# Row-tiled scatter and four-slot weight DMAs in the expert loop of a hybrid encoder layer with MoE

## Chip, cores and metric

One core of one Trainium2 chip. The metric is the device time of one launch in microseconds (us); lower is better. The kernel before has a median of 1183.3 us over 3 runs (1180.84 to 1186.23).

## What is computed

One layer on 256 tokens of width 1024, all in float32: RMSNorm, a mixer (projection, causal convolution, a complex linear recurrence, gates, output projection), then a top-4-of-32 mixture of experts, then a final RMSNorm. The change lies in the mixture of experts, which the reference gives per expert as:

```
gu = xb @ w_gate_up[e] + b_gate_up[e]            # (rows, 1024) @ (1024, 2048)
g, lin = gu[:, :1024], gu[:, 1024:]
g = jnp.minimum(g, 7.0); lin = jnp.clip(lin, -7.0, 7.0)
act = g * jax.nn.sigmoid(1.702 * g) * (lin + 1.0)
y = act @ w_down[e] + b_down[e]                  # (rows, 1024) @ (1024, 1024)
out[token] += gate[token, e] * y[row of token]
```

The weights of one expert are 8 MiB (w_gate_up) and 4 MiB (w_down); 32 experts make 384 MiB.

## The kernel before

Everything before the experts (mixer, router) takes about the first 270 us. After that comes a loop of 16 iterations with two experts each (`half` is 0 or 1), written out by hand in one order per engine; semaphores join the engines.

**The ring.** All weights pass through `ring`, 24 slots of 1 MiB (8 KiB in each of 128 partitions), 12 slots (`PER`) for each half. Slots 0 to 7 of a half hold one contraction block k of w_gate_up each, slots 8 to 11 hold two k of w_down each. The first two experts are loaded slot by slot ahead of the loop (`load`). Inside it SyncE (SP) waits for each two slots until the matmuls that read them have counted `chunk_used` up, and issues one DMA of 2 MiB for the expert two further on (`load_pair`, L355 to L361, called at L414 to L416); each pair of slots has a semaphore `pair_in`.

**TensorE (PE) for expert e** (L1316 to L1333): bias matmuls (L1272), `gate_up` for k = 0 to 3 (L1280), `gather` for the next expert (L1253, picks its tokens by a one-hot product), `gate_up` for k = 4 to 7, then `scatter` (L1298 to L1301), which adds the result of the expert before, `yrow`, to the output in PSUM banks 0 to 3, then `transposes` (L1259) of the activated rows `gc` and of the gathered rows, `spread_transposes` (L1264), and `down` (L1292). An expert has 64 rows. So that they use all 128 partitions of the outputs, gate_up, gather and down are column tiled: two matmuls with 64 columns each, `h` = 0 and 1, write partitions 0 to 63 and 64 to 127 of one bank, and the two run side by side. `yrow` therefore holds output columns 0 to 511 of the 64 rows in partitions 0 to 63 and columns 512 to 1023 in partitions 64 to 127. The scatter multiplies it with `spT`, the transposed matrix of gates. `spT` has a plane for each half of the columns, with zeros in the 64 partitions that belong to the other half, so each of the four matmuls (bank n: tokens n // 2, columns n % 2) runs over all 128 partitions.

**VectorE (DVE)** waits at L998 until gate_up is finished, clips the two halves (L969, L972), writes `spread` (L964), and makes the product (L975, L978). With L978 it releases PE's wait for `act_ready` at L1326. **ScalarE (ACT)** does the sigmoid (L658), copies PSUM to SBUF (L646, L649, L652, L655) and copies `spT` in two instructions (L662, L663), one for each 64 partitions.

After the loop PE scatters the last expert (L1366 to L1369), and ACT, DVE and SP make the final norm and store the output. A branch for experts with more than 64 rows (L1334 to L1363) is never entered with these inputs.

Of the kernel before, what the change touches and what calls it, by code (L numbers as in the profile page):

```python
# [26 lines left out]
D = 1024  # L27
T = 256
# [34 lines left out]
def build(nc, x, norm_mix_g, w_in, conv_w, conv_b, conv_ln_g, conv_ln_b, w_conv_out,  # L63
# [3 lines left out]
    with ExitStack() as ctx:  # L67
# [80 lines left out]
        gate = sb("gate", [128, TT, E + 1])  # L148
        pick = sb("pick", [128, TT, CAP])
        spread = sb("spread", [128, TT, 2, CAP])  # L150
        spT = sb("spT", [128, 2, TT, 128])
        biasb = sb("biasb", [96, 4 * 512], BF16)
        esel = sb("esel", [96, E + 1], BF16)
        onehot = sb("onehot", [96, 2, CAP], BF16)
# [43 lines left out]
        ffn_in = sem("ffn_in")  # L198
        down_in = sem("down_in")
        fin_in = sem("fin_in")  # L200
        pair_in = [sem(f"pair_in{i}") for i in range(SLOTS // 2)]
        stored = sem("stored")
        dve_own = sem("dve_own")
        pool_own = sem("pool_own")
# [102 lines left out]
        def _(sp):  # L307
# [38 lines left out]
            def load(e, j, half):  # L346

                if j < KD:
                    src, dst = gu_v[e, :, j, :], at(half * PER + j, CH)
                else:  # L350
                    c = j - KD
                    src, dst = dn_v[e, c // 2, :, c % 2 * 2:c % 2 * 2 + 2, :], grid(at(half * PER + j, CH), 2, D)
                sp.dma_start(dst, src).then_inc(pair_in[(half * PER + j) // 2], 16)

            def load_pair(e, j, half):  # L355

                if j < KD:
                    src, dst = gu_v[e, :, j:j + 2, :], grid(at(half * PER + j, 2 * CH), 2, CH)
                else:
                    src, dst = dn_v[e, (j - KD) // 2], grid(at(half * PER + j, 2 * CH), 4, D)  # L360
                sp.dma_start(dst, src).then_inc(pair_in[(half * PER + j) // 2], 16)  # L361

            sp.wait_ge(y_pe, ST)
            sp.dma_start(gffn, norm_ffn_g.to_broadcast([128, D])).then_inc(ffn_in, 16)
# [40 lines left out]
            with sp.Fori(0, E // 2 - 1) as i:  # L405
                for half in range(2):
                    e = i * 2 + half
                    with sp.If(any_more > 0):
                        over = sp.value_load(nums[0:1, bass.ds(e, 1)], min_val=0, max_val=1)
                        with sp.If(over > 0):  # L410
                            before = sp.value_load(nums[0:1, bass.ds(e + E, 1)], min_val=0, max_val=E)
                            sp.wait_ge(step, before * MORE_STEPS + MORE_STEPS + 1)
                            sp.sem_inc(passed, 1)
                    for j in range(0, PER, 2):  # L414
                        sp.wait_ge(chunk_used, e * PER + j + 2)
                        load_pair(e + 2, j, half)  # L416
            sp.wait_ge(chunk_used, E * PER - PER)
            sp.dma_start(at(0, D), norm_final_g.unsqueeze(0).to_broadcast([128, D])).then_inc(fin_in, 16)
            for t in range(TT):
# [7 lines left out]
        def _(pool):  # L427
# [99 lines left out]

            g.memset(rank[:, :, E:E + 1], -1.0).then_inc(consts, 1)
            g.memset(gate[:, :, E:E + 1], 0.0).then_inc(consts, 1)
            g.memset(spT[:, :, :, :], 0.0).then_inc(spT_sb, 1)  # L530
            pool.wait_ge(y_pe, ST)
            g.memset(ones, 1.0).then_inc(consts, 1)
            link(g.memset(tri, 1.0))
# [6 lines left out]
        def _(act):  # L540
# [118 lines left out]

            def spread_copy():  # L660

                s.activation(spT[0:64, 0, :, :], grid(bank[5][0:64, 0:T], 2, 128), ACT.Copy)  # L662
                return s.activation(spT[64:128, 1, :, :], grid(bank[5][64:128, 0:T], 2, 128), ACT.Copy)  # L663

            act.wait_ge(h_pe, 1)
            h_row_copy().then_inc(h_row, 1)
# [373 lines left out]
        def _(pe):  # L1040
# [226 lines left out]
            def gate_up(half, buf, part=None, uses=None):  # L1267

                ks = range(KD) if part is None else range(4 * part, 4 * part + 4)
                for b in range(2 if 0 in ks else 0):  # L1270
                    for h in range(2):
                        mm(bank[4 + b][64 * h:64 * h + 64, :], onehot[:, buf, :], biasb[:, (2 * b + h) * 512:(2 * b + h + 1) * 512],  # L1272
                           start=True, stop=False)
                for k in ks:
                    if uses is not None and k % 2 == 0:
                        pe.wait_ge(pair_in[(half * PER + k) // 2], uses)
                    w = at(half * PER + k, CH)
                    for b in range(2):
                        for h in range(2):
                            last = mm(bank[4 + b][64 * h:64 * h + 64, :], heT[:, k % 4, k // 4 * 64:k // 4 * 64 + 64],  # L1280
                                      w[:, b * FF + h * 512:b * FF + h * 512 + 512], start=False, stop=(k == KD - 1))
                    if uses is not None:
                        last.then_inc(chunk_used, 1)
                return last

            def down(half, uses=None):
                for k in range(KD):
                    if uses is not None and k % 4 == 0:
                        pe.wait_ge(pair_in[(half * PER + KD + k // 2) // 2], uses)
                    w = grid(at(half * PER + KD + k // 2, CH), 2, D)  # L1290
                    for h in range(2):
                        last = mm(bank[6][64 * h:64 * h + 64, :], actT[:, k % 4, k // 4 * 64:k // 4 * 64 + 64],  # L1292
                                  w[:, k % 2, h * 512:h * 512 + 512], start=(k == 0), stop=(k == KD - 1))
                    if uses is not None and k % 2:
                        last.then_inc(chunk_used, 1)
                return last

            def scatter():  # L1298
                for n in range(4):
                    last = mm(bank[n][:, :], spT[:, n % 2, n // 2, :], yrow, start=False, stop=False, skip_group_check=True)  # L1300
                return last  # L1301

            pe.wait_ge(gmT_sb, 1)
# [11 lines left out]
            with pe.Fori(0, E // 2) as i:  # L1315
                for half in range(2):  # L1316
                    e = i * 2 + half
                    pe.wait_ge(h_T, e + 1)
                    pe.wait_ge(spT_sb, e + 1)
                    gate_up(half, half, 0, i * 16 + 32)  # L1320
                    pe.wait_ge(pick_ready, e + 2)
                    pe.wait_ge(y_row, e + 1)
                    gather().then_inc(h_pe, 1)
                    gate_up(half, half, 1, i * 16 + 32)
                    scatter()
                    pe.wait_ge(act_ready, e + 1)  # L1326
                    transposes(gc, 4).then_inc(aT_pe, 1)
                    pe.wait_ge(h_row, e + 2)
                    transposes(hrow, 7).then_inc(hT_pe, 1)
                    pe.wait_ge(spread_ready, e + 1)  # L1330
                    spread_transposes().then_inc(spT_pe, 1)
                    pe.wait_ge(a_T, e + 1)
                    down(half, i * 16 + 32)  # L1333
                    with pe.If(any_more > 0):  # L1334
                        over = pe.value_load(nums[0:1, bass.ds(e, 1)], min_val=0, max_val=1)
                        with pe.If(over > 0):
                            before = pe.value_load(nums[0:1, bass.ds(e + E, 1)], min_val=0, max_val=E)
                            pe.wait_ge(y_row, e + 2)
                            pe.sem_inc(passed, 1)
                            with pe.Fori(0, MORE) as b:  # L1340
                                o = before * MORE_STEPS + b * BLOCK_STEPS + 1
                                pe.wait_ge(step, o)
                                scatter().then_inc(step, 1)
                                pe.wait_ge(step, o + 2)
                                gather().then_inc(step, 1)
                                pe.wait_ge(step, o + 4)
                                transposes(hrow, 7)
                                spread_transposes().then_inc(step, 1)
                                pe.wait_ge(step, o + 6)
                                gate_up(half, half).then_inc(step, 1)  # L1350
                                pe.wait_ge(step, o + 11)
                                transposes(gc, 4).then_inc(step, 1)
                                pe.wait_ge(step, o + 13)
                                down(half).then_inc(step, 1)
                            a = before * MORE_STEPS + MORE * BLOCK_STEPS + 1
                            pe.wait_ge(step, a)
                            scatter().then_inc(step, 1)
                            pe.wait_ge(step, a + 2)
                            gather().then_inc(step, 1)
                            pe.wait_ge(step, a + 4)  # L1360
                            transposes(hrow, 7).then_inc(step, 1)
                            pe.wait_ge(step, a + 6)
                            pe.sem_inc(passed, 1)  # L1363
            pe.wait_ge(y_row, E + 1)
            pe.wait_ge(spT_sb, E + 1)
            for t in range(TT):  # L1366
                for h in range(2):
                    last = mm(bank[2 * t + h][:, :], spT[:, h, t, :], yrow, start=False, stop=True, skip_group_check=True)
                last.then_inc(x2_pe, 1)  # L1369


# [18 lines left out]
```

## Time and profile before

| | |
|---|---|
| median of 3 runs | 1183.3 us (1180.84 to 1186.23) |
| the profiled execution, its own time | 1182.04 us |
| its span, first to last instruction | 1180.2 us |
| PE busy | 1126.3 us, 95% |
| DVE, ACT, POOL busy | 316.7, 179.1, 95.8 us |
| moved by DMA | 431.89 MB, mean 366 GB/s |
| mean granted TensorE clock | 0.972 of 2.4 GHz |

The profile is of one execution, and all times in it count from the first instruction. Its own time is 1.8 us above its span. Matmul records have modelled ends and overlap each other; starts are what to compare. A busy engine is not by itself the bound: what counts is which wait ends last in the stretch in question. "Granted clock" is 1.00 for 2.4 GHz and 0.50 for 1.2 GHz.

### The profile page before, as it was taken

The numbers are of one execution on the slowest core, as the hardware profiler recorded it, in microseconds if no ns is written. First come the engines' busy times: TensorE is split into PE (matmuls) and PEld (weight loads), VectorE is DVE, ScalarE is ACT, GpSimd is POOL, SyncE is SP. The second block draws the span as 40 slices with busy tenths as digits, with TensorE's granted clock in tenths as the row PEclk, the third lists the DMA queues.
The fourth block names the chain that finished last, engine by engine and source line by source line (L and its number), as shares of the span: only waits on it lengthen the run. The fifth ranks groups of instructions, "written<-read, shape, count | busy, mean of one in ns | idle before, by whom it ended". The sixth has DMA issues, their size and how long they took to land.

```text
span 1180.2 us, 12748 instructions
## 1 busy us (share of the span) xinstructions
PE 1126.3 (95%) x4959; PEld 497.7 (42%) x4960; DVE 316.7 (27%) x661; ACT 179.1 (15%) x333; POOL 95.8 (8%) x155
## 2 busy tenths in 40 slices
PE   7977769989999999999999999999999999999997
PEld 6855658553333333333333333333333333333332
DVE  3999996131111111111111111111111111111112
ACT  3100113111111111111111111111211111111112
POOL 2992520000000000000000000000000000000000
PEclk9987889979999999999999999999999999999999
DMA  8834018957999999999999999999999999999994
GB/s 230 255 98 179 1 38 350 386 214 294 411 416 419 428 429 428 429 429 428 428 429 429 428 429 428 429 428 428 428 429 429 428 429 429 429 428 428 428 429 206
DMA packets 51619, 431.89 MB, mean 366 GB/s; under 512 B 6466, under 2 KB 22256, under 8 KB 25391
## 3 DMA queue, kind: packets, MB, share of 16 engines
q1 hardware_dynamic: 51598, 431.62, 88.2%
q8 instruction: 12, 0.20, 0.1%
q14 instruction: 9, 0.07, 0.0%
HBM read 430.56 MB, written 1.05 MB: 366 GB/s over the span
## 4 chain that ended last, share of the span: by engine, by line
PE 81%; DVE 11%; DMA 5%; SPq 2%; issue 1%; ACT 1%; DVEq 0%; POOL 0%
PE bank L1280 34%; PE bank L1292 18%; PE bank L1300 9%; DVE ring L812 7%; PE bank L1253 4%; DMA ring<-w_gate_up 4%; PE bank L1259 3%; PE bank L1078 3%; PE bank L1215 2%; PE bank L1180 2%; SPq L361 1%; PE bank L1272 1%; DVE ring L844 1%; DVE ring L845 1%; DVE ring L835 1%
## 5 line engine op out<-in xcount | busy, mean ns | idle before, releaser
L1280 PE MATMUL bank<-ring,area 128*64 128x512 f32 x2048 | 451.7, 593 | 0.3 <-DMA ring<-w_gate_up 0.3
L1280 PEld LDWEIGHTS bank<-ring,area 128*64 128x64 f32 x2048 | 147.3, 137 | 281.5 <-issue 274.8
L969 DVE TENSOR_SCALAR area<-bank 128x512 f32<-128x512 f32 x32 | 22.1, 692 | 769.4 <-PE bank L1280 769.4
L1292 PE MATMUL bank<-ring,area 128*64 128x512 f32 x1024 | 226.8, 595 | 1.0
L1292 PEld LDWEIGHTS bank<-ring,area 128*64 128x64 f32 x1024 | 70.6, 137 | 136.6 <-issue 128.0
L1300 PE MATMUL bank<-area,spT 128*128 128x512 f32 x256 | 118.4, 605 | 0.0
L1078 PE MATMUL bank<-area,ring 128*128 128x256 f32 x480 | 116.8, 406 | 1.2 <-DVE area L749 1.2
L1078 PEld LDWEIGHTS bank<-area,ring 128*128 128x128 f32 x480 | 97.7, 206 | 20.4 <-issue 3.6
L812 DVE SCALAR_TENSOR_TENSOR ring<-ring,spread 128x256 f32<-128x256 f32 x180 | 98.3, 620 | 0.0
L658 ACT ACTIVATE area<-area 128x512 f32<-128x512 f32 x32 | 20.1, 630 | 497.3 <-DVE area L969 497.3
L1300 PEld LDWEIGHTS bank<-area,spT 128*128 128x128 f32 x256 | 46.0, 189 | 71.9 <-issue 71.9
L1253 PE MATMUL bank<-rows,pick 128*64 128x512 f32 x264 | 63.6, 604 | 0.0
L655 ACT ACTIVATE area<-bank 128x512 f32<-128x512 f32 x32 | 19.1, 597 | 193.7 <-PE bank L1292 193.7
L1259 PEld LDWEIGHTS bank<-ident,area 128*128 128x128 f32 x260 | 27.8, 141 | 26.0 <-DVE area L978 25.2
L1253 PEld LDWEIGHTS bank<-rows,pick 128*64 128x64 f32 x264 | 19.2, 139 | 39.3 <-issue 39.3
L1259 PE MATMUL bank<-ident,area 128*128 128x128 f32 x260 | 35.6, 280 | 0.0
L978 DVE TENSOR_TENSOR area<-area 128x512 f32<-128x512 f32 x32 | 33.7, 1053 | 1.1
L652 ACT ACTIVATE area<-bank 128x512 f32<-128x512 f32 x32 | 19.1, 597 | 76.7 <-PE bank L1259 76.7
L1215 PE MATMUL bank<-ring 128*128 128x512 f32 x64 | 28.1, 594 | 0.0
L1095 PE MATMUL bank<-area,ring 32*128 32x256 f32 x32 | 9.5, 480 | 17.0 <-ACT ring L584 17.0
L1272 PE MATMUL bank<-biasb,onehot 96*64 96x512 bf16 x128 | 19.8, 387 | 2.6 <-issue 2.6
L975 DVE SCALAR_TENSOR_TENSOR area<-area 128x512 f32<-128x512 f32 x32 | 21.9, 684 | 0.0
(240 smaller groups left out, 575.0 us busy)
## 6 DMA issues: line engine op xcount, KB each, us to landing
ring<-w_gate_up SPq DMA_DIRECT2D x120, 2048.0 KB, 29.9
ring<-w_down SPq DMA_DIRECT2D x60, 2048.0 KB, 28.3
ring<-w_gate_up SPq DMA_DIRECT2D x16, 1024.0 KB, 12.0
ring<-w_in SPq DMA_DIRECT2D x15, 1024.0 KB, 9.6
ring<-w_down SPq DMA_DIRECT2D x8, 1024.0 KB, 13.1
ring<-w_out SPq DMA_DIRECT2D x1, 4096.0 KB, 14.0
ring<-w_conv_out SPq DMA_DIRECT2D x1, 3072.0 KB, 13.3
rows<-x SPq DMA_DIRECT2D x2, 512.0 KB, 3.7
```

What stands on the lines that cost most here:

```text
L812: ins = v.scalar_tensor_tensor(conv[:, k, :], src, taps[:, k, w:w + 1], conv[:, k, :], ALU.mult, ALU.add)
L969: return v.tensor_scalar(gc, bank[4][:, :], 7.0, None, ALU.min)
L978: return v.tensor_tensor(gc.rearrange("a (m p) -> a p m", p=128), grid(lc, 128, 4), grid(sg, 128, 4), ALU.mult)
L1078: last = mm(bank[4 + n % 4][:, m * T:m * T + T], w[:, k, m * 128:m * 128 + 128], hT[:, k, :], start=(k == 0), stop=(k == KD - 1))
L1180: last = mm(bank[4 + j][:, m * T:m * T + T], wconv[:, k, c:c + 128], silu[:, k, :], start=(k == 0), stop=(k == KC - 1))
L1215: last = mm(bank[2 * t + h][:, :], gateC[:, k, t * 128:t * 128 + 128], wout[:, k, h * 512:h * 512 + 512], start=False, stop=(k == KD - 1))
L1253: last = mm(bank[6][64 * h:64 * h + 64, :], pick[:, t, :], rows[:, t, h * 512:h * 512 + 512], start=(t == 0), stop=(t == TT - 1))
L1259: last = tr(bank[b][:, m * 128:m * 128 + 128], src[:, m * 128:m * 128 + 128], ident[:, :])
L1272: mm(bank[4 + b][64 * h:64 * h + 64, :], onehot[:, buf, :], biasb[:, (2 * b + h) * 512:(2 * b + h + 1) * 512], start=True, stop=False)
L1280: last = mm(bank[4 + b][64 * h:64 * h + 64, :], heT[:, k % 4, k // 4 * 64:k // 4 * 64 + 64], w[:, b * FF + h * 512:b * FF + h * 512 + 512] ...
L1292: last = mm(bank[6][64 * h:64 * h + 64, :], actT[:, k % 4, k // 4 * 64:k // 4 * 64 + 64], w[:, k % 2, h * 512:h * 512 + 512], start=(k == ...
L1300: last = mm(bank[n][:, :], spT[:, n % 2, n // 2, :], yrow, start=False, stop=False, skip_group_check=True)
```

## The change

1. In the loop SP waits for four slots and issues one DMA of 4 MiB: k = 0 to 3, then k = 4 to 7 of w_gate_up (32 KiB in one run for each partition, 16 KiB before), then the whole w_down of the expert (two runs of 16 KiB for each partition). PE waits for four slots at a time, on `quad_in`.
2. `spT` has one plane of 128 partitions without zeros; ACT copies it with one instruction.
3. The scatter is row tiled: bank n uses only the 64 partitions of `spT` and `yrow` that hold its columns, 0 to 63 for even n and 64 to 127 for odd n. The final scatter does the same.

```diff
-        spT = sb("spT", [128, 2, TT, 128])
+        spT = sb("spT", [128, TT, 128])
...
-            def load_pair(e, j, half):
+            def load_quad(e, j, half):
 
                 if j < KD:
-                    src, dst = gu_v[e, :, j:j + 2, :], grid(at(half * PER + j, 2 * CH), 2, CH)
+                    src, dst = gu_v[e, :, j:j + 4, :], grid(at(half * PER + j, 4 * CH), 4, CH)
                 else:
-                    src, dst = dn_v[e, (j - KD) // 2], grid(at(half * PER + j, 2 * CH), 4, D)
-                sp.dma_start(dst, src).then_inc(pair_in[(half * PER + j) // 2], 16)
+                    src, dst = dn_v[e].rearrange("h p m n -> p h m n"), grid(at(half * PER + j, 4 * CH), 2, 4, D)
+                sp.dma_start(dst, src).then_inc(quad_in[(half * PER + j) // 4], 16)
...
-                    for j in range(0, PER, 2):
-                        sp.wait_ge(chunk_used, e * PER + j + 2)
-                        load_pair(e + 2, j, half)
+                    for j in range(0, PER, 4):
+                        sp.wait_ge(chunk_used, e * PER + j + 4)
+                        load_quad(e + 2, j, half)
...
-                s.activation(spT[0:64, 0, :, :], grid(bank[5][0:64, 0:T], 2, 128), ACT.Copy)
-                return s.activation(spT[64:128, 1, :, :], grid(bank[5][64:128, 0:T], 2, 128), ACT.Copy)
+                return s.activation(spT[:, :, :], grid(bank[5][:, 0:T], 2, 128), ACT.Copy)
...
-                    if uses is not None and k % 2 == 0:
-                        pe.wait_ge(pair_in[(half * PER + k) // 2], uses)
+                    if uses is not None and k % 4 == 0:
+                        pe.wait_ge(quad_in[(half * PER + k) // 4], uses)
...
-                    if uses is not None and k % 4 == 0:
-                        pe.wait_ge(pair_in[(half * PER + KD + k // 2) // 2], uses)
+                    if uses is not None and k == 0:
+                        pe.wait_ge(quad_in[half * 3 + 2], uses)
...
+            def scatter_half(n, stop=False):
+
+                r = slice(n % 2 * 64, n % 2 * 64 + 64)
+                return mm(bank[n][:, :], spT[r, n // 2, :], yrow[r, :], start=False, stop=stop, skip_group_check=True)
+
             def scatter():
                 for n in range(4):
-                    last = mm(bank[n][:, :], spT[:, n % 2, n // 2, :], yrow, start=False, stop=False, skip_group_check=True)
+                    last = scatter_half(n)
...
-                    last = mm(bank[2 * t + h][:, :], spT[:, h, t, :], yrow, start=False, stop=True, skip_group_check=True)
+                    last = scatter_half(2 * t + h, stop=True)
```

On SP, the six DMAs of an expert in the loop become three. Before:

```order
L361 ISA
L361 DMA ring<-w_gate_up 128x4096
L415 REGISTER_ALU
L361 ISA
L361 DMA ring<-w_gate_up 128x4096
...
L361 ISA
L361 DMA ring<-w_down 128x4096
L415 REGISTER_ALU
L361 ISA
L361 DMA ring<-w_down 128x4096
```

and now (each "ISA" row here is the wait for `chunk_used`):

```order
L361 ISA
L361 DMA ring<-w_gate_up 128x8192
L415 REGISTER_ALU
L361 ISA
L361 DMA ring<-w_gate_up 128x8192
L415 REGISTER_ALU
L361 ISA
L361 DMA ring<-w_down 128x2x4096
```

The order of the rows is the same; each DMA has moved behind the wait for two more slots.

## Rows read from the trace of the kernel before

**Rows 1.** The page: busy time, granted clock by slices, the chain by engine
```profile
PE 1126.3 (95%) x4959; PEld 497.7 (42%) x4960; DVE 316.7 (27%) x661; ACT 179.1 (15%) x333; POOL 95.8 (8%) x155
...
PEclk9987889979999999999999999999999999999999
...
PE 81%; DVE 11%; DMA 5%; SPq 2%; issue 1%; ACT 1%; DVEq 0%; POOL 0%
```
**Rows 2.** The chain in order of time (start us, length us): three starts of down
```profile
320.23 7.09 PE bank L1292 x32
...
352.40 7.09 PE bank L1292 x32
...
687.28 7.09 PE bank L1292 x32
```
**Rows 3.** Timeline (start us, us, instruction), PE and DVE between gate_up and down
```profile
710.19 3.70 PE L1300 MATMUL bank<-area,spT 128*128 128x512 f32 x8
...
713.85 1.09 PE L1259 MATMUL bank<-ident,area 128*128 128x128 f32 x8
...
715.19 7.09 PE L1292 MATMUL bank<-ring,area 128*64 128x512 f32 x32
...
710.30 0.69 DVE L969 TENSOR_SCALAR area<-bank 128x512 f32<-128x512 f32 x1 [24.08 <-PE bank L1280]
...
712.74 1.06 DVE L978 TENSOR_TENSOR area<-area 128x512 f32<-128x512 f32 x1
```
**Rows 4.** Windows (stretch: us, busy PE PEld DVE ACT POOL, clock, DMA share, GB/s)
```profile
204.00:228.00 24.00, 24.00 (x81) 15.19 (x80) 2.76 (x4) 0.00 (x0) 0.00 (x0) 1.00 1.02 421
...
692.00:720.00 28.00, 27.97 (x130) 10.15 (x128) 3.79 (x9) 3.43 (x7) 0.00 (x0) 1.00 1.01 428
```
**Rows 5.** SP's queue, L361: the first pair of the loop, then the sixth
```profile
L361 SPq DMA_DIRECT2D ring<-w_gate_up x1: 357/357/357, 275.6 to 275.6; - x1
...
DMA to landing us min/median/max: 8.5/8.5/8.5
...
L361 SPq DMA_DIRECT2D ring<-w_down x1: 333/333/333, 299.6 to 299.6; - x1
...
DMA to landing us min/median/max: 10.9/10.9/10.9
```
**Rows 6.** Timeline of PE, the last expert; in brackets idle before, and its releaser
```profile
1149.73 3.60 PE L1280 MATMUL bank<-ring,area 128*64 128x512 f32 x16
1153.64 3.65 PE L1280 MATMUL bank<-ring,area 128*64 128x512 f32 x16 [0.31 <-DMA ring<-w_gate_up]
1157.22 3.70 PE L1300 MATMUL bank<-area,spT 128*128 128x512 f32 x8
...
1162.22 7.09 PE L1292 MATMUL bank<-ring,area 128*64 128x512 f32 x32
1170.01 3.70 PE L1368 MATMUL bank<-area,spT 128*128 128x512 f32 x8 [0.70 <-ACT area L655]
```
**Rows 7.** Timeline of PE at three waits, with the row-tiled matmuls of L1095
```profile
49.66 6.85 PE L1078 MATMUL bank<-area,ring 128*128 128x256 f32 x31
56.45 1.14 PE L1095 MATMUL bank<-area,ring 32*128 32x256 f32 x8
58.81 1.98 PE L1095 MATMUL bank<-area,ring 32*128 32x256 f32 x8 [1.22 <-ACT ring L584]
...
11.06 1.19 PE L1078 MATMUL bank<-area,ring 128*128 128x256 f32 x2 [1.15 <-DVE area L749]
...
329.87 1.06 PE L1272 MATMUL bank<-biasb,onehot 96*64 96x512 bf16 x4 [2.56 <-issue]
```
**Rows 8.** Windows of PE alone at these waits (us, PE busy, clock, DMA share, GB/s)
```profile
59.90:63.20 3.30, 3.30 (x10) 0.50 0.40 135
...
8.60:12.00 3.40, 2.13 (x6) 1.00 0.84 176
...
329.60:332.90 3.30, 3.03 (x10) 0.50 1.03 437
```

More of the change, by code:

```diff
@@ L200, in build @@
         fin_in = sem("fin_in")
-        pair_in = [sem(f"pair_in{i}") for i in range(SLOTS // 2)]
+        quad_in = [sem(f"quad_in{i}") for i in range(SLOTS // 4)]
         stored = sem("stored")
@@ L352, in load @@
                     src, dst = dn_v[e, c // 2, :, c % 2 * 2:c % 2 * 2 + 2, :], grid(at(half * PER + j, CH), 2, D)
-                sp.dma_start(dst, src).then_inc(pair_in[(half * PER + j) // 2], 16)
-            def load_pair(e, j, half):
+                sp.dma_start(dst, src).then_inc(quad_in[(half * PER + j) // 4], 16)
+            def load_quad(e, j, half):
                 if j < KD:
-                    src, dst = gu_v[e, :, j:j + 2, :], grid(at(half * PER + j, 2 * CH), 2, CH)
+                    src, dst = gu_v[e, :, j:j + 4, :], grid(at(half * PER + j, 4 * CH), 4, CH)
                 else:
-                    src, dst = dn_v[e, (j - KD) // 2], grid(at(half * PER + j, 2 * CH), 4, D)
-                sp.dma_start(dst, src).then_inc(pair_in[(half * PER + j) // 2], 16)
+                    src, dst = dn_v[e].rearrange("h p m n -> p h m n"), grid(at(half * PER + j, 4 * CH), 2, 4, D)
+                sp.dma_start(dst, src).then_inc(quad_in[(half * PER + j) // 4], 16)
             sp.wait_ge(y_pe, ST)
@@ L529, in _ @@
             g.memset(gate[:, :, E:E + 1], 0.0).then_inc(consts, 1)
-            g.memset(spT[:, :, :, :], 0.0).then_inc(spT_sb, 1)
+            g.memset(spT[:, :, :], 0.0).then_inc(spT_sb, 1)
             pool.wait_ge(y_pe, ST)
@@ L1319, in _ @@
                     pe.wait_ge(spT_sb, e + 1)
-                    gate_up(half, half, 0, i * 16 + 32)
+                    gate_up(half, half, 0, i * 16 + 64)
                     pe.wait_ge(pick_ready, e + 2)
@@ L1323, in _ @@
                     gather().then_inc(h_pe, 1)
-                    gate_up(half, half, 1, i * 16 + 32)
+                    gate_up(half, half, 1, i * 16 + 64)
                     scatter()
@@ L1332, in _ @@
                     pe.wait_ge(a_T, e + 1)
-                    down(half, i * 16 + 32)
+                    down(half, i * 16 + 64)
                     with pe.If(any_more > 0):
```

## The prediction

> **What bounds the kernel now.** I read the page first. PE is busy 95% of the span, the clock row has 9 in every slice from the 300th microsecond on, and PE alone makes 81% of the chain [rows 1]. That says where to look, not what an edit is worth, so the chain in order of time is next: down starts at 687.28 and again at 715.19 [rows 2, 3], so an expert takes 27.91 us, and the chain repeats this from 352 us on to the last expert without another engine in it. The loop runs at PE's pace. The windows give the second clock. A stretch in mid-loop moves 428 GB/s at a DMA share of 1.01 [rows 4]: the 16 DMA engines are full. An expert's 12 MiB are 12.58 MB, and 12.58 / 0.428 = 29.4 us. So **DMA is 1.5 us an expert slower than PE**, and the kernel lives on its ring: PE starts with two experts loaded and eats up its lead. At the very end the lead is just used up: PE waits 0.31 us for a w_gate_up DMA at 1153.64, and nowhere in the loop before [rows 6]. Two chains of almost the same length end there together, PE's with 32 x 27.91, and DMA's.
>
> Third, what stands between gate_up and down inside an expert [rows 3]. Scatter starts at 710.19; its 8 records (4 matmuls, two passes each) stand 0.43 apart by their 3.70 less about 0.2 of pipeline end, so PE is occupied until 713.6. Beside it DVE works off its chain from 710.30 and ends L978 at 713.80. The transposes start at 713.85, **0.05 us behind DVE**, not behind the scatter. The scatter fills a wait which PE has anyway.
>
> **The change, part by part.**
>
> *The scatter.* Row tiled, banks 0 and 1 use different rows of the array and can run side by side, as can 2 and 3. The nearest row is L1095, whose matmuls use 32 rows at a time: 8 records of 256 columns in 1.14 us, 0.14 each, where full ones of this width take 6.85 / 31 = 0.22 [rows 7]. So float32 row tiles do overlap. The scatter falls from 3.44 to about 1.72 us, 1.72 x 32 = 55 us of PE's busy time. On the path this gives nothing: the transposes wait for L978, 3.6 us after gate_up ended, as before. In its place PE gets a wait: from 1.72 to 3.66 us, **1.9 us idle in each expert**. The drain between tiling shapes is not new, gate_up to scatter changes shape now too. After the loop the final scatter has no DVE beside it: ACT starts on banks 0 and 1 as soon as both are ready, and they come 0.86 us sooner: -0.9 us.
>
> *The clock.* The new wait may cost what the scatter saved. The rows have waits of this size on both sides. After 1.22 us without work between two groups of narrow matmuls the granted clock went to 0.50, 1.2 GHz, for 3.3 us; after 1.15 us between full ones it stayed at 1.00; after 2.56 us in the loop it went to 0.50, again for 3.3 us [rows 7, 8]. The fall inside the loop has a price: the downs start at 320.23 and 352.40, 32.17 apart [rows 2], 4.26 above the period; 2.56 of this is the wait, so the fall is **1.7 us**. 1.9 us lies between the waits that went both ways (1.15, 1.22) and the one that fell (2.56), and behind it come only short transposes (1.5 us with gaps), so it is nearer to the bad end. Bounds: no fall, 0; a fall in each of 32 experts, 54 us. I take every second expert, 16 x 1.7 = +27 us, since the same gap can be met or missed by a clock that is not in step with the loop.
> The Trainium skill (TensorE: Matmul & The Clock Gate, "Why this matters for your kernels") speaks for the other end: a wait of under 2 us is shorter than what it warns of. By its rule this term would be 0. Row 1.22 here already contradicts it, though with narrow matmuls around.
>
> *Coarser DMAs, the start.* The ring is full and the DMA engines are empty when the loop begins; the first pair is issued at 275.6. A DMA of four slots can go only when the fourth is used, 3.4 us later. The third one (w_down) cannot go before 299.6, where the sixth pair went before; that pair landed 10.9 later, at 310.5 [rows 5]. A pair alone takes 8.5, which is 4.9 of transfer (2.10 MB / 0.428) and 3.6 around it; four slots then take 9.8 + 3.6 = 13.4 and land at 313.0. So DMA's chain is **2.5 us later**, and about 0.5 more is lost in the next two experts, where the queue again just runs dry before w_down is released; later it has ever more ahead of it. Taken: +3.0; bounds 2.3 and 5.
>
> *Coarser DMAs, the end.* The last expert's k = 6 and 7 were released at 1153.64. Now k = 4 needs the whole DMA too, which lands at 1153.6 + 3.0 = 1156.6, and could have started at 1149.73 [rows 6]. From 1156.6 it takes 6.9 to the end of gate_up, 1163.5 for 1157.2: +6.3 us, if PE is there in time and the rate of DMA stays. w_down then lands 9.8 behind 1156.6, 1166.4, while down is reached 5.0 after gate_up's end, at 1168.5: no further wait. But with 16 clock falls PE reaches k = 4 at 1149.7 + 27 = 1177, when all has long landed: in my forecast this term is **0**, hidden by the slower PE.
>
> *The rate.* 1 MiB DMAs with runs of 8 KiB made 421 GB/s, 2 MiB with 16 KiB 428 [rows 4]: 0.04 us less per MiB. If doubling again gives half of that, 0.02 x 240 (w_gate_up alone) to 0.02 x 360 (all) = 5 to 7 us off DMA's chain; below, nothing. Again this is worth something only where DMA sets the end.
> The Trainium skill (DMA: Bandwidth & Descriptors, "Measured") has a much steeper curve, 341 GB/s for 1 MB and 425 for 16 MB, of single transfers. The queued ones here show 421 at 1 MiB, so the row decides, and what is left to win is small.
>
> *Small things.* ACT copies spT in one instruction for two of 0.37, off the path, since its reader is a whole gate_up later. SP issues 90 DMAs for 180. The 2.56 us wait for instructions at 329.87 stays; if fetching queues behind longer transfers, up to as much again. PE's 0.31 at 1153.64 goes.
>
> **Sum**, against the profiled execution's own 1182.0 (its span 1180.2 and 1.8 around it; it is 1.3 below the median): +27.2 - 0.9 - 0.3 = **1208 us**.
>
> **The rivals.**
> 1. *The clock holds, and the longer runs pay.* DMA's chain is 3 us later and 5 to 7 shorter, k = 4 of the last expert waits 0 to 2 us instead of 0.31, and PE's 32 x 27.91 sets the end: 1182.0 - 0.9 + up to 1.7, **1182**, no change. This is the other sign. It decides between 1.9 us of wait and the clock: below some length nothing falls, and rows have 1.15 without a fall. Against it, 1.22 with one.
> 2. *The clock holds, the rate stays at 428.* Then the end waits for DMA: 1182.0 + 6.3 - 0.9 = **1187.4**, +0.46%. For it, the 428 is already flat over the whole loop.
> 3. *Every expert falls.* Period 27.91 + 1.7 = 29.6, above DMA's 29.4: 1182 + 54 - 1 = **1235**. For it, the transposes behind the wait are light work too.
> 4. *The row tiles do not run side by side* (the change does not do what it says). Scatter stays 3.44, nothing idles, and rival 1 or 2 holds without the -0.9. Against it, L1095.
>
> **Chances.** Some but not all experts fall, 1195 to 1230: 0.55. Rival 3: 0.07. Rival 1: 0.20. Rival 2: 0.10. Rival 4: 0.05. Something that gains over 0.5%: 0.03, since no row has a way for PE's chain to get shorter by 6 us. The likeliest is the first, whose own range is 1195 to 1230. The range must reach rivals 1 and 2: 1180 to 1228. A measurement here can tell about 0.5%, 5.9 us. Slower by more: 0.55 + 0.07 + 0.04 of rivals 2 and 4 = 0.66. Within: 0.30. Faster: 0.04.
>
> **What would show it.** Scatter: eight records in about 1.9 us, then a wait of PE for DVE L978 near 1.9 us in every expert, and L1259 still 3.66 behind the scatter's start; if that is nearer, DVE was not the bound. Clock: the slices of the granted clock fall from 1.00 to about 0.94 in the loop (16 x 3.3 us of 900); if all stand at 1.00, the forecast is wrong and the time is that of rival 1 or 2. The distance of two downs is 27.9 without and 29.6 with a fall. DMA: GB/s in mid-loop 428 or up to 433, the third DMA of the loop landing near 313, and the wait for w_gate_up in the last expert 0 (forecast), 2 (rival 1) or 7 us (rival 2). Waits on DMA before the last five experts would mean that I have DMA's chain wrong.

## The result and the profile after

The changed kernel takes 1190.72 us in the median of 12 runs (1182.72 to 1198.24), the kernel before 1183.55 in the 12 beside them (1180.84 to 1186.23). The ratio is 1.0058, with a 95% interval of 1.0034 to 1.0082: slower by about 7 us, where 25 had been forecast. What is new is not only the median. The runs of before lie within 5.4 us, those of the change within 15.5. The profiled execution is the second shortest of the twelve: 1184.94 us, span 1183.1.

The page of the changed kernel, as in [rows 1]:

```profile
PE 1077.1 (91%) x4959; PEld 476.2 (40%) x4960; DVE 316.1 (27%) x661; ACT 167.5 (14%) x301; POOL 95.6 (8%) x155
...
PEclk9987889979999999999999999999999999999999
...
PE 77%; DVE 19%; issue 2%; ACT 1%; DMA 0%; DVEq 0%; SPq 0%; POOL 0%; ACTq 0%
```

PE is busy 49 us less (1126.3 before), and the time did not fall. DVE has 19% of the chain for 11%, since between gate_up and down the chain now runs through DVE's instructions, where before it ran through the scatter. The timeline of the same place as [rows 3] shows it:

```profile
711.26 1.99 PE L1300 MATMUL bank<-area,spT 64*128 64x512 f32 x8
714.89 1.09 PE L1258 MATMUL bank<-ident,area 128*128 128x128 f32 x8 [1.65 <-DVE area L977]
...
716.24 7.09 PE L1291 MATMUL bank<-ring,area 128*64 128x512 f32 x32
```

The row tiles do run side by side: eight records in 1.99 us for 3.70. The transposes start 3.63 behind the scatter's start, as before (3.66), since DVE ends its chain no sooner, and PE idles 1.65 us by the modelled end of the last record. The slices of the clock row show nothing, but the chain in order of time (start, length) does:

```profile
1022.98 7.09 PE bank L1291 x32
1039.08 6.89 PE bank L1279 x32
1050.86 8.78 PE bank L1291 x32
...
1136.24 8.78 PE bank L1291 x32
```

Two of 32 downs take 8.78 in place of 7.09 us. They are three experts apart. The windows of PE alone, laid on these two places, give the reason (columns as in [rows 8]):

```profile
1051.20:1054.50 3.30, 3.30 (x10) 0.50 1.04 447
1136.60:1139.80 3.20, 3.20 (x10) 0.50 1.09 471
```

So the granted clock does fall behind the new wait, the fall costs 1.70 us (downs 29.58 apart for 27.88), and it happened twice, not 16 times. The rest of this execution's difference of 2.9 us: its loop begins 1.5 us later (first gate_up at 273.23 for 271.77; from 262 to 275 us its mean granted clock was 0.71 for 0.76), the end is 0.7 shorter (from the last down to the end of the span it takes 17.28 for 17.98), before's last expert was 0.5 longer than the others by its wait for DMA, and an expert takes 27.885 us for 27.906, 0.7 us over the loop.

DMA, in the mid-loop window as in [rows 4], and the third DMA of the loop as in [rows 5], the first w_down:

```profile
692.00:720.00 28.00, 26.32 (x130) 9.37 (x126) 3.77 (x9) 3.07 (x6) 0.00 (x0) 1.00 1.00 431
```
```profile
L361 SPq DMA_DIRECT2D ring<-w_down x1: 384/384/384, 301.0 to 301.0; - x1
...
DMA to landing us min/median/max: 13.9/13.9/13.9
```

It lands at 314.9; without the 1.5 of later loop start 313.4, 2.9 behind the 310.5 of before. The rate is 431 for 428 GB/s. PE waits for no weight DMA in this execution: the last w_gate_up lands at 1153.4, and PE, held up by two falls, asks for it at 1153.87.

What one trace can't tell, how many falls the other eleven executions had, can be read roughly from the mean granted clock of each. In order of time, the five shortest have 0.964 to 0.972, the next two 0.963 and 0.965, the five longest 0.957 to 0.960. In the three kernels below that have no falls in their traces (e1, e3, e11) it is 0.966 to 0.973, with a median of 0.971. One fall, 3.3 us at half the clock, is worth 0.0014. So the median execution, at 0.964, had about five falls, and the longest nine or ten. These are estimates: what the clock does ahead of the loop also moves the mean, by up to 0.005.

### The profile page after: what moved, and what is told of

Read it like the earlier page. It is cut to its first block, busy times and chain, and to the rows that moved or that the text cites. A ratio compares the mean times of both kernels' runs of the same rounds, so it can differ in the third digit from the quotient of the medians.

```text
span 1183.1 us, 12356 instructions
## 1 busy us (share of the span) xinstructions
PE 1077.1 (91%) x4959; PEld 476.2 (40%) x4960; DVE 316.1 (27%) x661; ACT 167.5 (14%) x301; POOL 95.6 (8%) x155
## 4 chain that ended last, share of the span: by engine, by line
PE 77%; DVE 19%; issue 2%; ACT 1%; DMA 0%; DVEq 0%; SPq 0%; POOL 0%; ACTq 0%
PE bank L1279 37%; PE bank L1291 19%; DVE ring L811 7%; PE bank L1252 5%; PE bank L1258 3%; DVE area L977 3%; PE bank L1077 3%; PE bank L1214 2%; DVE area L971 2%; PE bank L1179 2%; DVE area L974 2%; DVE spread L963 1%; PE bank L1271 1%; DVE ring L843 1%; DVE ring L844 1%
## 5 line engine op out<-in xcount | busy, mean ns | idle before, releaser
L1077 PE MATMUL bank<-area,ring 128*128 128x256 f32 x480 | 119.2, 412 | 1.2 <-DVE area L748 1.2
L1300 PE MATMUL bank<-area,spT 64*128 64x512 f32 x264 | 65.6, 615 | 0.7 <-ACT area L655 0.7
L1300 PEld LDWEIGHTS bank<-area,spT 64*128 64x128 f32 x264 | 22.7, 186 | 43.1 <-issue 41.5
## 6 DMA issues: line engine op xcount, KB each, us to landing
rows<-x SPq DMA_DIRECT2D x2, 512.0 KB, 3.8
```

Source lines behind the costliest of these rows:

```text
L1077: last = mm(bank[4 + n % 4][:, m * T:m * T + T], w[:, k, m * 128:m * 128 + 128], hT[:, k, :], start=(k == 0), stop=(k == KD - 1))
L1300: return mm(bank[n][:, :], spT[r, n // 2, :], yrow[r, :], start=False, stop=stop, skip_group_check=True)
```

## Experiments

**What belongs to which part.** The first four kernels take the parts one by one. Ratios are to runs of before taken beside each kernel.

Coarser DMAs with the scatter of before:

```diff
-        spT = sb("spT", [128, TT, 128])
+        spT = sb("spT", [128, 2, TT, 128])
...
-                return mm(bank[n][:, :], spT[r, n // 2, :], yrow[r, :], start=False, stop=stop, skip_group_check=True)
+                return mm(bank[n][:, :], spT[:, n % 2, n // 2, :], yrow, start=False, stop=stop, skip_group_check=True)
```

> Four-slot DMAs with the full-height scatter of before. Theory A (the time and the spread come from clock falls at the new 1.9 us wait of the row-tiled scatter): 1181 to 1186, median within 3 us of before (1183.6), spread as narrow as before (5 us), no fall to 0.50 in the loop but the one at the first turn. Theory B (the coarser DMAs delay the end, by 5 to 7 us): 1188 to 1191, and PE waits for w_gate_up in the last experts.

Measured: 1186.71 us (1184.2 to 1189.44, 12 runs), ratio 1.0028 (1.0011 to 1.0045), no fall in the loop but the one at its first turn. Neither theory alone: the spread is the 5 us of theory A, but 3 us are lost, and the trace has theory B's waits, smaller than expected. The timeline of PE in this kernel:

```profile
1124.95 7.09 PE L1280 MATMUL bank<-ring,area 128*64 128x512 f32 x32 [0.91 <-DMA ring<-w_gate_up]
...
1154.19 7.09 PE L1280 MATMUL bank<-ring,area 128*64 128x512 f32 x32 [0.92 <-DMA ring<-w_gate_up]
```

The last three intervals between downs are 29.21, 29.21 and 29.24 for 27.90: 1.3 each, 4.0 us with the 0.1 before them, against 0.5 in before's last. DMA's chain reaches PE three experts ahead of the end. It is hardly late by then. The last w_gate_up DMA of this kernel:

```profile
L361 SPq DMA_DIRECT2D ring<-w_gate_up x1: 332/332/332, 1103.0 to 1103.0; - x1
...
DMA to landing us min/median/max: 51.1/51.1/51.1
```

It lands at 1154.1, 882.1 behind the first gate_up (272.05); before's last pair landed at 1153.6, 881.8 behind its own (271.77). The late start of 2.9 us has been made up on the way. What differs is who needs it: PE wants it at k = 4, at 1154.19, where the kernel before needed its last pair only at k = 6, 3.4 us further on.

The row-tiled scatter alone, on the kernel before (the diff of the change without its lines on DMAs and waits):

> Row-tiled scatter with the pair DMAs of before. Theory A: median 1187 to 1192, single runs 1182 to 1198, each some multiple of 1.7 us above the lowest. Theory B: 1182 to 1184, as before less 0.9 for the final scatter.

Measured: 1191.71 us (1187.73 to 1195.42, 6 runs), ratio 1.0073 (1.0047 to 1.0098). Theory A holds for this part. This alone costs as much as the whole change (1.0058), a point that comes back below. The chain in order of time of this kernel:

```profile
574.05 8.78 PE bank L1291 x32
...
659.42 8.78 PE bank L1291 x32
...
744.78 8.78 PE bank L1291 x32
...
1086.21 8.78 PE bank L1291 x32
```

Seven falls, at 574, 659, 745, 830, 915, 1001 and 1086: none in the first ten experts, and from then on **every third one**, its down 85.36 us behind the one before.

The changed kernel with the wait filled:

```diff
+            def fill(n):
+                for _ in range(n):
+                    mm(bank[7][:, :], ident[:, :], rows[:, 0, 0:512], start=True, stop=True)
...
                     scatter()
+                    fill(2)
                     pe.wait_ge(act_ready, e + 1)
```

> The changed kernel with two full float32 matmuls (128 x 512, results never read) into bank 7 behind the row-tiled scatter, which fill PE's wait for DVE. Theory A: falls gone, 1181 to 1184, spread 5 us. Theory B: as the changed kernel, 1188 to 1192. Third theory (switching to row tiling itself disturbs PE): also 1188 to 1192, with wide spread.

Measured: 1185.20 us (1182.65 to 1189.09, 12 runs), ratio 1.0024 (1.0009 to 1.0039), no fall in the loop. Work that nobody reads makes the kernel faster than the changed one, by 5.5 us between the medians and 0.34% (4 us) between the ratios, whose intervals just touch, and takes the spread back to 6.4. The granted clocks say the same: 0.967 to 0.973 in all twelve. Row tiling as such is thereby cleared. One thing is mixed in: an expert takes 27.93 us here, not 27.89, which matters below; the kernel with half the wait filled has not that flaw. What is left above before is the 3 us of the DMAs, with two waits of 0.9 for w_gate_up in the trace.

A longer wait (the kernel leaves out the sums of banks 2 and 3, so its output is wrong):

```diff
-                    scatter()
+                    scatter_half(0)
+                    scatter_half(1)
```

> The changed kernel with only banks 0 and 1 scattered in the loop (the sums for tokens 128 to 255 are left out), so PE waits 2.8 us in each expert in place of 1.9. Theory A: falls in most experts, at 1.7 us each, 1215 to 1235. If the length of the wait is not what matters: as the changed kernel, 1183 to 1198.

Measured: 1201.4 us (1193.0 to 1205.86, 6 runs), ratio 1.0154 (1.0117 to 1.0191). More than with the shorter wait, less than expected. Its trace has eleven falls, the first behind the first expert, and again every third: the intervals between downs run 29.55, 27.89, 27.89, 29.55. The wait is 2.5 us by modelled ends, and it is not hit more often than one in three here either.

**Half the wait.** With `fill(1)` for `fill(2)`:

> The changed kernel with one full matmul in the wait in place of two: 1.1 us of idle PE is left. If a wait of 1.1 us never lowers the clock (as the 1.15 at the start of the trace of before): as with the filled wait, 1184 to 1187, narrow, no fall. If it can (as the 1.22 there): single runs up to 1199.

Measured: 1184.83 us (1182.93 to 1188.65, 12 runs), ratio 1.0019 (1.0005 to 1.0033), no fall. In the timeline the wait is now

```profile
713.33 1.09 PE L1258 MATMUL bank<-ident,area 128*128 128x128 f32 x8 [0.60 <-DVE area L977]
```

0.60 us by modelled ends, 1.1 between the end of the work and DVE's end by its cadence. The twelve granted clocks are 0.968 to 0.973. An expert takes 27.89 us, as in the changed kernel, so it is the length of the wait that made the difference: such a wait is harmless here.

**Why every third, and why not always.** Three intervals with one fall are 27.89 + 27.89 + 29.58 = 85.36. Do the falls follow the loop, or a beat of their own that the loop nearly meets? Windows of 0.05 us around the first and the last fall of the row tiles alone (PE alone, columns as in [rows 8]) tell them apart:

```profile
574.30:574.35 0.05, 0.05 (x2) 0.78 0.77 328
...
1086.30:1086.35 0.05, 0.05 (x2) 0.77 0.00 0
```

The clock drops at the same place of both windows, so 512.0 us lie between these falls, 85.33 for each three experts, while their downs start 512.16 apart (574.05 and 1086.21). In the half scatter it is the other way: its first fall lies at 291.98 and its last at 1145.31, ten steps of 85.33, while the downs behind them start 85.31 apart (292.22 and 1145.32). In both traces the falls keep a beat of their own. A hit then brings the third expert on to nearly the same place, and a run pays from its first hit to the end: up to 11 falls, 19 us. A run with a late first hit pays little; the profiled one had its first at the 28th expert. That fits the 15 us of spread. If so, another length of the expert breaks it. First try, a transposition into bank 7 between the first half of gate_up and the gather:

```diff
                     gate_up(half, half, 0, i * 16 + 64)
+                    for _ in range(1):
+                        tr(bank[7][:, 0:128], ident[:, :], ident[:, :])
```

> The changed kernel with one more 128-column transposition (result never read) between the first half of gate_up and the gather, so that an expert takes PE 0.107 us longer, 3.4 us over the loop. Theory E (falls need the expert to lie right against a fixed beat; at 27.885 us three experts and one fall make 85.33 and meet it again and again, and by laying the falls of two traces on one beat I count that 0.107 more breaks this and leaves 0 to 2 falls): FASTER in spite of the added work, median 1184 to 1187, spread as narrow as before, at most 2 falls in the trace. Theory F (each wait of 1.9 us has its chance, whatever the step of the loop): 3.4 slower than the changed kernel, 1192 to 1195, spread 15.

> As the one before with two such transpositions, 0.215 us an expert, 6.9 us over the loop. Theory E: falls are back, 2 to 7 of them, no longer every third expert; median 1190 to 1196, slower than with one. Theory F: 1195 to 1199.

Measured: 1198.24 us (1195.37 to 1199.85, 5 runs) with one, 1199.08 (1197.93 to 1200.08, 4 runs) with two. Both expectations missed, because the edit added more than I took it for. The intervals are 28.30 and 28.41 us: the first transposition costs 0.41, the second 0.11. In the timeline of the kernel with one, it takes 0.26 to the next start, and the rest lies around the change of shape:

```profile
703.60 7.04 PE L1279 MATMUL bank<-ring,area 128*64 128x512 f32 x32
710.56 0.33 PE L1326 MATMUL bank<-ident 128*128 128x128 f32 x1
710.82 1.94 PE L1252 MATMUL bank<-rows,pick 128*64 128x512 f32 x8
```

So 13 and 17 us of work were added. The times rose by 7.5 and 8.4 over the changed kernel, and the spreads shrank to 4.5 and 2.2. The traces have two falls each in the loop (intervals 29.99 and 30.00; 30.10 twice), not in threes, and the first has a further one in the last down. That speaks for the beat, but it did not test the length I had named. So the same with a pair of column-tiled matmuls, the shape of their neighbours:

```diff
+                    for h in range(2):
+                        mm(bank[7][64 * h:64 * h + 64, 0:64], ident[:, 0:64], ident[:, 0:64], start=True, stop=True)
```

> As the kernel with one more step, but the added work is a pair of column-tiled matmuls of 64 columns, the shape of their neighbours, so that an expert grows by 0.107 us and not by the 0.41 that the transposition cost. Theory E: 0 to 2 falls in the loop, not in threes, median 1185 to 1188 (3.4 us of added work, and no falls), spread 7 or less: faster than the changed kernel's 1190.7. Theory F (each wait of 1.7 us has its own chance of a fall, whatever the loop's step): 1191 to 1194, single runs spread over 15 us as those of the changed kernel.

> The same with 128 columns, 0.215 us an expert, 6.9 over the loop. Theory E: 2 to 7 falls, never every third expert; median 1191 to 1199, and well above the kernel with 64 columns, by 5 to 11 us where the work differs by 3.4. Theory F: 1194 to 1198, spread 15.

Measured: 1188.46 us (1186.53 to 1190.08, 6 runs), ratio 1.0048 (1.0035 to 1.0061), with 64 columns, and 1190.97 (1190.13 to 1192.72, 5 runs), ratio 1.0071 (1.0058 to 1.0084), with 128. The experts take 28.00 and 28.11 us, the traces have one fall (at 719) and three, none a third expert behind another. With 64 columns the kernel does 3.7 us more work than the changed one and its median is 2.3 lower, 0.5 above my bound; the two intervals overlap, so "faster" is likely rather than shown. What is clear is the spread, 3.6 and 2.6 us, and the granted clocks, 0.967 to 0.971 in all eleven runs, where theory F, the same chance for each wait, wanted the changed kernel's 15 us and its clocks down to 0.957. The step from 64 to 128 was 2.5 us, no more than its own work (3.4), and not the 5 or more that I expected from returning falls: my count from two traces was too high there. So the trains of falls at every third expert belong to the step of 27.89, seen in three kernels that have it (the changed one, the row tiles alone, the half scatter) and in none of the four with another. That rests on one trace for each kernel and on the clocks of 4 to 6 runs; where in its beat a given run starts was not controlled.

**Which part of the coarser DMAs costs 3 us.** On the filled kernel, w_down back in two DMAs:

```diff
-                    for j in range(0, PER, 4):
-                        sp.wait_ge(chunk_used, e * PER + j + 4)
+                    for j in (0, 4, 8, 10):
+                        sp.wait_ge(chunk_used, e * PER + j + (4 if j < KD else 2))
...
-                    if uses is not None and k == 0:
-                        pe.wait_ge(quad_in[half * 3 + 2], uses)
+                    if uses is not None and k % 4 == 0:
+                        pe.wait_ge(late_in[half] if k else quad_in[half * 3 + 2], uses)
```

> The kernel with the filled wait, and w_down again in two DMAs of 2 MiB (w_gate_up stays at 4 MiB). Theory C (the rest, 3 us above before with no clock fall, is DMA's chain, late because w_down of the first expert can be issued only when all four slots are used): the last w_gate_up lands 1.4 us sooner, PE's waits for it in the last experts shrink from 0.9 each to 0 to 0.5, time 1182 to 1184. Theory D (it is the wait of PE for four slots in place of two that costs): as the filled kernel, 1185.

Measured: 1185.66 us (1182.1 to 1187.9, 12 runs); beside its own runs of before (1184.37) the ratio is 1.0009 (0.9993 to 1.0025). Against the 1.0024 of the filled kernel that is a hint, with intervals that overlap. The last w_gate_up lands 880.7 us behind the first gate_up, 1.9 sooner than in the filled kernel (882.6), where theory C had 1.4. The trace has no wait of PE for a weight DMA at all, but its PE was also later: the first turn of the loop took 33.95 for 32.41 us, and every second expert 28.00 for 27.93, 1.0 us in all, in a step just ahead of down whose cause is open. And the reverse, on the kernel before, w_down alone in one DMA:

```diff
-                    src, dst = dn_v[e, (j - KD) // 2], grid(at(half * PER + j, 2 * CH), 4, D)
+                    src, dst = dn_v[e].rearrange("h p m n -> p h m n"), grid(at(half * PER + j, 4 * CH), 2, 4, D)
...
-                    for j in range(0, PER, 2):
-                        sp.wait_ge(chunk_used, e * PER + j + 2)
+                    for j in range(0, KD + 1, 2):
+                        sp.wait_ge(chunk_used, e * PER + j + (4 if j == KD else 2))
...
-                    if uses is not None and k % 4 == 0:
-                        pe.wait_ge(pair_in[(half * PER + KD + k // 2) // 2], uses)
+                    if uses is not None and k == 0:
+                        pe.wait_ge(pair_in[(half * PER + KD) // 2], uses)
```

> The kernel before, with w_down alone in one DMA of 4 MiB; w_gate_up in pairs, full-height scatter. Theory C (the 3 us come from w_down, which can only be issued when its four slots are used): DMA's chain 2.5 later from the first expert on, at the old rate of 428, so PE waits for w_gate_up in the last experts, 2 to 3 us in all: ratio to before 1.002. Theory D (they come from PE waiting for four slots of w_gate_up): as before, ratio 1.000.

Measured: 1186.82 us (1184.08 to 1191.84, 11 runs), ratio 1.0031 (1.0013 to 1.005). That is near theory C's 1.002, and w_down alone costs what all the coarser DMAs cost. Its mechanism is shown only in part. Every second expert takes 27.98 for 27.91 us, 1.0 us in all, ahead of down and without a wait for DMA. The last w_gate_up lands 885.9 us behind the first gate_up for 881.8 before, 4.1 later, of which 1.6 belong to this execution, whose clock was still at 0.50 when the loop began. And PE does not wait for w_gate_up, as theory C had it, but for w_down itself, which it now needs whole:

```profile
1140.56 7.09 PE L1292 MATMUL bank<-ring,area 128*64 128x512 f32 x32 [1.24 <-DMA ring<-w_down]
...
1170.04 7.09 PE L1292 MATMUL bank<-ring,area 128*64 128x512 f32 x32 [1.34 <-DMA ring<-w_down]
```

So a coarser DMA costs twice, by its late release and because its reader needs it whole. e5 shows the first (1.9 us of DMA's chain), the landings of e1 the second; no run separates them in the time.

**Something useful in the wait.** The gather of the next expert needs 1.72 us of PE and stood between the halves of gate_up. Behind the scatter it fills the wait for DVE:

```diff
                     gate_up(half, half, 0, i * 16 + 32)
-                    pe.wait_ge(pick_ready, e + 2)
-                    pe.wait_ge(y_row, e + 1)
-                    gather().then_inc(h_pe, 1)
                     gate_up(half, half, 1, i * 16 + 32)
+                    pe.wait_ge(y_row, e + 1)
                     scatter()
+                    pe.wait_ge(pick_ready, e + 2)
+                    gather().then_inc(h_pe, 1)
```

Once with the pair DMAs, once with those of the change, once with w_down in pairs:

> Pair DMAs, row-tiled scatter, and the gather of the next expert moved from between the halves of gate_up into the wait behind the scatter. An expert takes PE 26.2 us for 27.9, so DMA sets the pace (29.4): PE waits for it in every expert from about the 14th on. w_down is released 1.7 us sooner, so the hole of 1.8 us before the fifth pair goes: if DMA's chain is all that counts then, 1178 to 1181. If clock falls still reach the end: 1181 to 1185. If PE's chain were the bound alone, 1182 - 54 = 1128.

> The changed kernel with the gather moved into the wait behind the scatter. DMA sets the pace, at 430.7 GB/s: its chain gains 5.6 us over 90 DMAs against pairs and starts 1 us later; PE waits for whole quads. Expected 1177 to 1182, with a narrow spread, since a clock fall of 1.7 us fits into PE's 3 us of wait in each expert. If clock falls add to DMA's chain: 1183 to 1198, as the changed kernel.

> As the one before, with w_down in two DMAs. Theory C: 0 to 1 us faster than it (its first w_down lands sooner, at a slightly lower rate). Theory D: 1 to 3 us faster.

> The same kernel as e6_gather_in_wait_pairs, whose 12 runs held one of 1593 us beside eleven between 1177.8 and 1185.5. If that one was a disturbance from outside: again 1178 to 1182, ratio 0.996 to 0.998, and no run far above. If the order of the gather makes a rare long wait: again a run hundreds of us above.

Measured with pairs: 1179.93 us (12 runs, eleven from 1177.8 to 1185.53, one of 1593.08), ratio 0.9963 (0.9946 to 0.998), and again 1180.26 (1177.96 to 1182.81, 12 runs), ratio 0.9979 (0.9967 to 0.999). The run of 1593 is left out of the ratio and did not come again. Its mean granted clock was 0.651, that of the eleven others 0.966 to 0.974; why is open. An expert takes PE 26.54 us (26.2 expected), and from the 17th or 18th on (14th expected) DMA's 29.37. **This version beats the kernel before** in two series, by 0.2 to 0.4%. The timeline of PE in its last experts (second series):

```profile
1145.63 3.65 PE L1279 MATMUL bank<-ring,area 128*64 128x512 f32 x16 [1.15 <-DMA ring<-w_gate_up]
1150.52 3.65 PE L1279 MATMUL bank<-ring,area 128*64 128x512 f32 x16 [1.23 <-DMA ring<-w_gate_up]
1154.10 1.99 PE L1299 MATMUL bank<-area,spT 64*128 64x512 f32 x8
1156.02 1.94 PE L1252 MATMUL bank<-rows,pick 128*64 128x512 f32 x8
```

Scatter and gather now stand back to back, and the waits for DMA come in pieces of 1.2 us, which never lowered the clock in either trace. The other two were measured once, and their intervals too lie below before. With four-slot DMAs the same 3 us of waiting comes in fewer pieces, of up to 2.5 us: 1182.15 us (1180.05 to 1189.5), ratio 0.9983 (0.9967 to 0.9998); with w_down in pairs 1181.09 (1179.89 to 1187.18), ratio 0.9975 (0.9959 to 0.9991). Both traces have seven falls between 746 and 1160. In the four-slot version ten waits are of 2.4 to 2.5 us, and seven of them end in a fall, far more than one in three. Most are swallowed by DMA's pace, but one that meets the last expert is not. From the chain of the four-slot version:

```profile
1156.36 8.78 PE bank L1279 x32
```

The second half of the last gate_up took 8.78 for 6.89. The spread was 9.5 us and not narrow, as I had expected. That fall is 1.9 us of it; more lies ahead of the loop, since the execution with this fall, the longest of the twelve, began its loop at 276.38, 4.6 us later than the one of before. The difference between these two (0 to 1 or 1 to 3 expected) is within their intervals.

## Why the prediction was wrong

- **The scatter**: right. 3.44 to 1.72 us, nothing gained on the path, because L978 ends last; a wait of 1.9 us in its place (1.65 by modelled ends); 0.9 (0.7 measured in the tail) at the end.
- **The clock**: the mechanism and its price were right, the count was not. The step that failed is "I take every second expert, 16 x 1.7 = +27 us". A fall costs 1.70 us, but there were two in the trace and about five in the median execution (estimated above from 0.964 for 0.971 of granted clock), 8.5 us. I read the bounds from single waits of the trace and took the middle between 0 and 32. The runs show that the same wait in every expert is followed by a fall only in some, that the falls keep a beat of 85.33 us that is not the loop's, and that with experts of 27.89 us one hit makes a train. The remark that the clock is not in step with the loop was the wrong way round: with this expert they nearly are.
- **What the clock row would show** was worked out wrongly too: 16 x 3.3 us of 900 at half the clock lower its mean to 0.97, not to 0.94, and the slices show tenths. Both kernels have 9 in every slice of the loop, so that row could not tell the forecast from its rivals; the chain in order of time could.
- **The rule of longer waits**: the Trainium skill (TensorE: Matmul & The Clock Gate, "Why this matters for your kernels") warns only of longer waits than these. The traces do not agree: waits of 1.9 us were followed by a fall in 2 and in 7 of 32 experts, waits of 2.5 us in 11 of 32. By that rule the term would have been 0 and the time rival 1's, 1182. The measurement stands between the two; waits of 1.1 to 1.2 us inside the loop never had a fall, though the one of 1.22 in [rows 7] had.
- **DMA's start**: 2.5 us forecast for the third DMA, 2.9 measured. **The rate**: 431, within "428 or up to 433". From the third DMA to the last w_gate_up, DMA's chain took 838.5 us in the changed kernel and 840.5 in e1, for 843.1 between the same places before: 2.6 to 4.6 us shorter, between the 0 of rival 2 and the 5 to 7 of rival 1.
- **DMA's end**: "in my forecast this term is 0, hidden by the slower PE" was right wherever falls came. It was 0 in the profiled execution, and the row tiles alone (1.0073) cost no less than with the coarser DMAs (1.0058). Where no falls come it shows, 0.28% or 3.3 us (e1). Rival 1 had 0 to 2 us for the wait and rival 2 7, the trace 4.0 in steps of 1.3, in the last three to four experts only, as the prediction's last sentence allowed.
- **The number**: 1208 stood for a case that did not come. The range, 1180 to 1228, held the time, and the sign was right, but the 1190.7 lies below the 1195 to 1230 of the likeliest case and above the 1182 and 1187.4 of rivals 1 and 2.

So the 7 us are not the sum of 3.3 for DMAs and a rest for falls, since the two hide each other. They are about 8.5 us of falls in the median execution, less 0.7 at the end and about 1 for slightly shorter experts and before's own last wait. Filling the wait gains only 4 of them, since the DMAs then show.

## What to carry to other kernels

Before an engine's work is shortened, look at what the work behind it waits for: here the scatter filled a wait for DVE, and a gain came only when other needed work, the gather, was put in its place. On TensorE an empty stretch can cost more than itself, so here the same total of waiting was cheaper in pieces of about 1 us than of 2. When a kernel's times spread more after a change than before, compare the intervals of the loop turn by turn in one trace before comparing medians; and where transfers fill a ring as fast as it is used, a coarser DMA is issued later and its reader needs it whole: here that took back what the higher rate gave, and 3 us more.

## What the hardware showed unexpectedly

- Falls of the clock in trains: every third expert at an interval of 27.89 us, 85.33 us apart, seven times in a row in one trace and eleven in another; single ones, one to three in a trace, at 28.00, 28.11, 28.30 and 28.41.
- One 128-column transposition between column-tiled matmuls cost 0.41 us, a second one behind it 0.11.
- In its first turn the loop has a wait of PE for which the profile shows no cause (2.56 us before). In the traces it cost between 2.5 and 6.1 us, depending on whether falls followed: 29.08 for 26.54 in the second series of the best kernel, 34.14 for 28.00 in the kernel with 64 more columns. Only the half scatter's trace has no such wait.
- The start of the loop lay between 270.7 and 276.4 us in these traces, with the granted clock ahead of it: from 262 to 275 us its mean was 0.80 in the earliest, 0.76 in the one of before and 0.50 in the two latest. This range of 5.7 us is about the 5.2 to 6.4 us by which the twelve runs of kernels without falls differ; that the one makes the other is not shown.
